# First layer's neighbourhood attention: query tiles of 8 rows by 16 columns, key blocks of 12 rows by 32 columns

## The chip, the cores and the metric

The kernel runs on one core of a Trainium2 chip. The metric is the device time of one execution in microseconds. Before the change it is 2199.93 us, the median of three runs (2194.26 to 2201.35).

## What is computed

Two layers over 1,024 latent tokens (a grid of 16 rows by 64 columns) and 256 context tokens, width 1,024. In each layer one input projection gives q, k, v and a gate z; a mixer gives y; `(y * silu(z)) @ w_out` is added to the stream and normalised. The first layer's mixer is a neighbourhood attention with 16 heads of 64. A query at row r, column w sees 8 rows by 16 columns of keys, clamped to the grid, and all 256 context keys:

```
row_start = clip(r - 4, 0, 16 - 8)
col_start = clip(w - 8, 0, 64 - 16)
s_loc = q . k_win * scale + rpb[h, r0 + i - r + 7, col_start + j - w + 15]
s_ctx = q . kc * scale
p = softmax(concat(s_loc, s_ctx))
y = p_loc @ v_win + p_ctx @ vc
```

Context queries attend to context keys alone. The second layer is a differential attention over all keys, with a rotary embedding on latent tokens.

## The kernel before

The first layer's projection and attention run in eight chunks of two heads. In a chunk PE makes twelve products (four blocks v, k, q, gate; three groups of 512, 512 and 256 tokens; L450), each in three passes over high and low parts of h and w. The v block is transposed tile by tile (L461), k and q are split into high and low parts on DVE (`split_k`, `split_q` L602, L606). Four products of the next chunk run at the end of a chunk (`ahead`).

**Items.** An item is one head and one tile of 128 queries: two rows of 64 columns. Per head there are eight local items and two of context queries, 20 items a chunk. A local item's keys are the 8 or 9 full rows that its two query rows' windows cover, 512 or 576 keys, besides 256 context keys. So it has 1,536 or 1,664 score columns (each key twice, for k's high and low part) in six matmuls (L907), a key block of 128 is transposed on PE (L917) and evacuated by ACT (L802), and multiplied with v (L930, two records for each block): 6 or 7 blocks.

DVE takes the maximum (L837) of the context scores, adds the bias to the local ones and takes their maximum in one instruction (L843), joins both maxima (L846), and after ACT's exponential (L795) takes the reciprocal (L852) and multiplies (L855). PE's order in iteration i is: scores of item i+2, first part of the transposes of i, first values of i-1, second transposes, second values. DVE's order is: normalise i, maximum of i+2. The scores of an item wait for the exponential of the item two before. `gate_y` (L862) multiplies the finished y with half the gate.

**Bias.** A table expanded in DRAM (`toeplitz`, 14 of 16 heads at the start of this stage, by POOL's queue, L220) holds for each query column a row of relative biases. For each chunk two DMAs (`load_bias`, L736) bring two heads of it into `aux`; four additions on POOL (L777, L781) put the window's mask on it. DVE waits for these (`bias_ready`) before the first maximum of a chunk.

**SP's queue.** It is strictly in order. In a chunk: late modulation loads 3 to 5 (`late.load`, L252), the next chunk's first weight block (L409), loads 6 and 7, the store of the modulation row (L283), three weight blocks, the next chunk's loads 0 to 2, then the wait for the last maximum of the chunk, `load_bias` of the next one, the wait for y, y's store (L756). The late modulation multiplies a part of w_mod with the condition on DVE, in two parts (loads 0 to 2 at the head of a chunk, 3 to 7 ahead of `split_q`; L261, L265); PE reduces it (L272) after the ninth product and before the two early gate products. The order of the start of this stage is: masks, `load_bias(0)`, weight blocks 2 and 3, late loads.

```
sp.wait_ge(max_done, CREDIT + c * NI + NI)
load_bias(c + 1)
...
sp.wait_ge(y_ready, CREDIT + c * YG + YG)
sp.dma_start(y_out[bass.ds(c * P, P), :], m.y[:, :]).then_inc(y_stored, 16)
```

## Time and profile before

| what | value |
|---|---|
| median of three runs | 2199.93 us (2194.26 to 2201.35) |
| span of the profiled execution | 2192.7 us |
| instructions in it | 32,602 |
| busy share of the span | PE 91%, DVE 59%, ACT 42%, POOL 6% |
| first layer's projection and attention, eight chunks | 941 us |
| granted TensorE clock, mean | 0.969 |

The profile lists the span of its execution, from the first to the last instruction; the times of the three runs also hold what lies around the span. Busy time of an engine is the time in which at least one of its instructions ran; matmuls overlap, so a matmul's own duration is longer than the distance to the next one's start. A bracket behind a row gives the idle time before it and what ended it. SPq is the DMA queue of SyncE; its rows are the issue of a transfer, not the transfer.

### The profile page before, as it was taken

To read this page: it belongs to the slowest core of one execution; us is meant where nothing else is said; L and a number is where in the kernel's file an instruction comes from. 1 tells how busy PE (TensorE), PEld (TensorE's weight loads), DVE (VectorE), ACT (ScalarE), POOL (GpSimd) and SP (SyncE) were. 2 spreads that over 40 slices of the span, in tenths; PEclk is the share of its full clock that TensorE was granted. 3 is DMA by queue.
4 is the path that set the end of the run, shared out by engine and by line. 5 is a ranking of instruction groups with operands and counts; after the bars stand their busy time and mean duration, and the time that the engine had idled before them with its cause. 6 is when DMAs were issued, how large, how long until landed. Compare 5 with 4: busy or idle time off the path is not lost. (4 is left out here: it accounts for less than half of the span.)

```text
span 2192.7 us, 32602 instructions
## 1 busy us (share of the span) xinstructions
PE 1985.7 (91%) x11889; PEld 1705.5 (78%) x11889; DVE 1292.7 (59%) x2330; ACT 921.9 (42%) x1544; POOL 138.0 (6%) x123
## 2 busy tenths in 40 slices
PE   7799999999999898997977999999999999998687
PEld 2688888888888888886766787878787878787566
DVE  2474646465564646475764748474747474747557
ACT  1353444435362625263113545454545454545410
POOL 0301010100001010100100000000000000000010
PEclk9899999999999999998988999999999999999889
DMA  7512111121212021114532000000000000001142
GB/s 281 152 30 77 29 58 47 41 65 41 65 36 66 27 64 41 53 59 143 190 111 88 20 29 19 29 19 29 19 29 19 29 19 29 19 20 39 48 173 96
DMA packets 99168, 134.07 MB, mean 61 GB/s; under 512 B 5152, under 2 KB 70848, under 8 KB 98992
## 3 DMA queue, kind: packets, MB, share of 16 engines
q1 hardware_dynamic: 89984, 101.05, 14.6%
q0 software_dynamic: 6544, 22.95, 3.4%
q10 hardware_dynamic: 2592, 9.44, 1.1%
q8 instruction: 30, 0.49, 0.1%
q14 instruction: 18, 0.15, 0.0%
HBM read 114.50 MB, written 22.84 MB: 63 GB/s over the span
## 5 line engine op out<-in xcount | busy, mean ns | idle before, releaser
L450 PE MATMUL acc<-h_hi,w_hi 128*128 128x512 f32 (+1 forms) x1408 | 518.6, 368 | 14.6 <-DVE w_lo L432 14.6
L450 PE MATMUL acc<-h_hi,w_lo 128*128 128x512 f32 (+1 forms) x1408 | 509.7, 362 | 0.0
L450 PE MATMUL acc<-h_lo,w_hi 128*128 128x512 f32 (+1 forms) x1408 | 509.0, 361 | 0.0
L450 PEld LDWEIGHTS acc<-h_hi,w_hi 128*128 128x128 f32 x1408 | 267.3, 190 | 60.0 <-DVE w_lo L432 15.4
L450 PEld LDWEIGHTS acc<-h_hi,w_lo 128*128 128x128 f32 x1408 | 266.6, 189 | 41.7
L450 PEld LDWEIGHTS acc<-h_lo,w_hi 128*128 128x128 f32 x1408 | 267.3, 190 | 37.9
L930 PE MATMUL acc<-pt,v 128*128 128x128 f32 x1792 | 247.4, 277 | 0.0
L802 ACT ACTIVATE pt<-acc 128x512 f32<-128x512 f32 (+2 forms) x288 | 143.5, 502 | 229.9 <-PE acc L917 229.3
L930 PEld LDWEIGHTS acc<-pt,v 128*128 128x128 f32 x1792 | 224.3, 194 | 0.2 <-ACT pt L802 0.2
L1156 PE MATMUL acc<-k_dup,q_stack 128*128 128x512 f32 (+1 forms) x768 | 185.5, 382 | 38.3 <-DVE q_stack L606 24.5
L1085 DVE TENSOR_REDUCE stats<-acc 128x1 f32<-128x1280 f32 x128 | 189.9, 1487 | 46.4 <-PE acc L1156 46.4
L1156 PEld LDWEIGHTS acc<-k_dup,q_stack 128*128 128x128 f32 x768 | 140.6, 198 | 78.6 <-issue 24.4
L917 PE MATMUL acc<-ident,big 128*128 128x128 f32 x896 | 147.8, 278 | 47.9 <-DVE big L855 47.8
L1177 PE MATMUL acc<-pt,v 128*128 128x128 f32 x1280 | 175.6, 278 | 0.8
L1034 ACT ACTIVATE pt<-acc 128x512 f32<-128x512 f32 (+1 forms) x192 | 100.7, 524 | 156.2 <-PE acc L1165 153.6
L1177 PEld LDWEIGHTS acc<-pt,v 128*128 128x128 f32 x1280 | 161.2, 194 | 3.2 <-issue 2.1
L1027 ACT ACTIVATE big<-acc,stats 128x1280 f32<-128x1280 f32 x96 | 127.5, 1328 | 72.1 <-DVE stats L1085 70.4
L917 PEld LDWEIGHTS acc<-ident,big 128*128 128x128 f32 x896 | 106.4, 142 | 62.7 <-issue 28.5
L795 ACT ACTIVATE big<-acc,stats 128x768 f32<-128x768 f32 (+2 forms) x160 | 133.3, 833 | 25.9 <-DVE stats L846 25.9
L907 PE MATMUL acc<-k_dup,q_stack 128*128 128x256 f32 (+1 forms) x832 | 139.1, 300 | 0.0
L1165 PE MATMUL acc<-ident,big 128*128 128x128 f32 x640 | 104.2, 278 | 25.7 <-DVE big L1098 23.9
L432 DVE TENSOR_TENSOR w_lo<-w_raw,w_hi 128x1024 fp32r<-128x1024 f32 x64 | 78.2, 1224 | 68.7 <-ACT w_hi L427 68.0
(146 smaller groups left out, 2556.5 us busy)
## 6 DMA issues: line engine op xcount, KB each, us to landing
w_raw<-in_w_in SPq DMA_DIRECT2D x64, 512.0 KB, 4.0
extra_prob<-in_w_mod SPq DMA_DIRECT2D x40, 256.0 KB, 3.1
w_raw<-y_t POOLq DMA_DIRECT2D x18, 512.0 KB, 5.6
w_raw<-in_w_out SPq DMA_DIRECT2D x16, 512.0 KB, 3.3
aux<-toeplitz SPq DMA_DIRECT2D x16, 448.0 KB, 5.6
big<-in_w_mod SPq DMA_DIRECT2D x24, 256.0 KB, 3.0
y_t<-y SPq DMA_DIRECT2D x8, 640.0 KB, 3.3
x<-big ACTq DMA_DIRECT2D x10, 512.0 KB, 2.6
```

Of the source, the lines that this page charges most:

```text
L450: mm = nc.tensor.matmul(m.bank(self.bank_of(j), w), wt[:, b % 2, k, :], ht[:, k, t0:t0 + w], start=(k == 0 and i == 0), stop=(k == KT - 1 ...
L795: nc.scalar.activation(prob[:, i % PB, 0:it.width], m.banks(2 * (i % 2), 0, it.width), ACT.Exp, bias=stat(i, 2), accum_out=stat(i, 3)).the ...
L802: nc.scalar.activation(m.pt[:, n % 3, 0:w], m.bank(4 + n % 2, w), ACT.Copy).then_inc(pt_ready, 1)
L907: mm = nc.tensor.matmul(m.psum[:, b, col:col + w], m.q_stack[:, it.head, it.qt * P:(it.qt + 1) * P], m.k_dup[:, it.head, part, key:key + w ...
L917: mm = nc.tensor.transpose(m.psum[:, 4 + n % 2, t * P:(t + 1) * P], prob[:, i % PB, (a + t) * P:(a + t + 1) * P], m.ident[:, :])
L930: mm = nc.tensor.matmul(m.psum[:, 6 + it.y_group % 2, (it.qt % 4) * P:(it.qt % 4 + 1) * P], m.v[:, it.key_tiles[a + t], :], m.pt[:, n % 3, ...
L1027: nc.scalar.activation(prob(mp, t), m.banks(3 * mp, 0, TOK), ACT.Exp, bias=stat(t, mp), accum_out=stat(t, 2 + mp)).then_inc(exp_done, 1)
L1034: nc.scalar.activation(m.pt[:, n % 4, 0:w], m.bank(6, w), ACT.Copy).then_inc(pt_ready, 1)
L1085: nc.vector.reduce_max(stat(t, mp), m.banks(3 * mp, 0, TOK), AX, negate=True).then_inc(max_done, 1)
L1156: mm = nc.tensor.matmul(m.bank(3 * mp + g, w), m.q_stack[:, mp, t * P:(t + 1) * P], m.k_dup[:, mp, part, k0:k0 + w], start=(part == 0), st ...
L1165: mm = nc.tensor.transpose(m.psum[:, 6, i * P:(i + 1) * P], prob(0, t)[:, (a + i) * P:(a + i + 1) * P], m.ident[:, :])
L1177: mm = nc.tensor.matmul(m.psum[:, 7, (t % 4) * P:(t % 4 + 1) * P], m.v[:, a + i, :], m.pt[:, n % 4, i * P:(i + 1) * P], start=(a + i == 0) ...
```

## The change

Query tiles become 8 rows by 16 columns, and each has one key block of 12 rows by 32 columns, 384 keys in three blocks of 128, in place of 512 or 576. Latent tokens are stored in cells of 4 rows by 8 columns (the host permutes x and the output, and the rotary table), so that a key block is three runs of 128 tokens, and q is regrouped by tile as it is split. v is transposed for each of the 16 places at which a block of 4 rows by 32 columns can start: 18 tiles a chunk in place of 10, in five groups (`v_turns`); they lie partly in `big`.

The scores lie in one bank (local, 384) and the next (context, 256), next to each other, so the maximum is: add of the bias over 384, then one reduction over 640. Transposes come in parts of 3 and 2 blocks. The factor 0.5 moves from `gate_y` to the evacuation of v.

The bias table in DRAM becomes eight shifted copies cut into strips of 8 columns (`shifted`), written by 8 + 8 DMAs in 32-byte pieces. For each chunk 64 DMAs of 8 partitions (48 pieces of 384 bytes each) bring it in. Masks shrink to one row and one column mask; POOL puts them on with 20 additions a chunk: sixteen that also move strips to their place (4 of 4 or 2 strips of 96 elements for each of four head and row pairs, 8 of 384 elements and 8 of 192) and four over 1,152 elements.

```diff
-PAD = 63 - (WIN_C - 1)
-RPB_W = 2 * WIN_C - 1 + 2 * PAD
-RPB_H = 2 * WIN_R - 1
-SLOTS = RPB_H - 1
-INNER = WIN_R + 1
+Q_ROWS, Q_COLS = 8, 16
+K_ROWS, K_COLS = 12, 32
+LOCAL = K_ROWS * K_COLS
+BAND, STRIP = 4, 8
+CELL = BAND * STRIP
+BANDS, STRIPS = ROWS // BAND, GRID_W // STRIP
+BAND_TOKENS = BAND * GRID_W
+ROW_BLOCKS, COL_BLOCKS, KINDS = ROWS // Q_ROWS, GRID_W // Q_COLS, 3
+K_BAND0 = [0, 1]
+K_STRIP0 = [0, 1, 3, 4]
+KIND = [0, 1, 1, 2]
+SLOT = [0, 8, 4]
+LOADED_AT, LOADED = 4, 6
+MOVES = [(0, 0, 4), (1, 2, 2), (1, 0, 2), (2, 0, 4)]
+K_BANDS, K_STRIPS = K_ROWS // BAND, K_COLS // STRIP
+PAD_R, PAD_C = 4, 16
+RPB_H = 2 * WIN_R - 1 + 2 * PAD_R
+RPB_W = 2 * WIN_C - 1 + 2 * PAD_C
+SHIFTS = (RPB_W + 1 - STRIP) // STRIP
...
-def expand_band(pool, rpb, toeplitz, h, bands):
-
-    src = rpb[h, :, 63:127]
-    pool.dma_start(toeplitz[h].rearrange("w d j -> d w j"),
-                   bass.AP(src.tensor, src.offset, [[RPB_W, RPB_H], [-1, GRID_W], [1, GRID_W]])).then_inc(bands, 16)
...
+def expand_bias(pool, rpb, shifted, heads, bands):
+
+    for c in range(STRIP):
+        src = rpb[heads, :, STRIP - 1 - c:2 * STRIP - 1 - c]
+        rows = (heads.stop - heads.start) * RPB_H
+        pool.dma_start(shifted[c, :, heads.start * RPB_H:heads.stop * RPB_H, :],
+                       bass.AP(src.tensor, src.offset, [[STRIP, SHIFTS], [RPB_W, rows], [1, STRIP]])).then_inc(bands, 16)
...
+        if l == 0:
+            self.v_turns = [(b // 2, [b * BAND_TOKENS + s0 * CELL for s0 in K_STRIP0]) for b in range(BANDS)]
+            self.v_turns += [(2, [SEQ, SEQ + P])]
+        else:
+            self.v_turns = [(g, range(t0, t0 + w, P)) for g, (t0, w) in enumerate(GROUPS)]
+        self.NV = len(self.v_turns)
+        self.turned_by = [max(i for i, t in enumerate(self.v_turns) if t[0] == g) + 1 for g in range(3)]
...
+        for n in range(2, self.NV - 1):
+            self.turn_v(pe, c, n)
+        if self.NV > 3:
+            self.product(pe, c, AHEAD + 1)
+        self.turn_v(pe, c, self.NV - 1)
+        for j in range(AHEAD + (2 if self.NV > 3 else 1), self.cum[2]):
...
+            if self.l == 0 and g < ROW_BLOCKS:
+                by_cell = lambda t: t.rearrange("p (r b n) -> p r b n", r=2, n=2 * CELL)
+                by_block = lambda t: t.rearrange("p (b r n) -> p r b n", r=2, n=2 * CELL)
+            else:
+                by_cell = by_block = lambda t: t
+            src = lambda rows: by_cell(m.y[rows, t0:t0 + w])
+            dst = lambda rows, h: by_block(m.q_stack[rows, h, t0:t0 + w])
...
-    def __init__(self, head, qt):
-        self.head, self.qt = head, qt
-        self.local = qt < LAT_TILES
-        self.rows = 0
+    def __init__(self, head, n):
+        self.head, self.n = head, n
+        self.local = n < LAT_TILES
         if self.local:
-            r = 2 * qt
-            start = [min(max(x - WIN_R // 2, 0), ROWS - WIN_R) for x in (r, r + 1)]
-            self.k0 = start[0]
-            self.rows = start[1] + WIN_R - start[0]
-            self.slot = self.k0 - r + WIN_R - 2
-        self.width = CTX + self.rows * GRID_W
-        tiles = [LAT_TILES + i for i in range(CTX_TILES)]
-        if self.local:
-            tiles += [self.k0 // 2 + i for i in range((self.rows + 1) // 2)]
-        self.key_tiles = tiles
-        self.y_group = head * 3 + qt // 4
-
-
-def neighbourhood(nc, m, stack, p, out_w, rpb, toeplitz, bands, masks_in, w_mod, mod_rows, y_out):
+            self.col, self.row = n // 2, n % 2
+            self.kind = KIND[self.col]
+            self.blocks = [(K_BAND0[self.row] + b) * COL_BLOCKS + self.col for b in range(K_BANDS)]
+        else:
+            self.blocks = []
+        self.blocks += [BANDS * COL_BLOCKS + i for i in range(CTX_TILES)]
+        self.width = len(self.blocks) * P
+        self.y_group = head * 3 + n // 4
+
+    def queries(self, q):
+        pos = (self.row * COL_BLOCKS + self.col) if self.local else self.n
+        return q[:, pos * P:(pos + 1) * P]
+
+    def keys(self, k):
+        first = K_BAND0[self.row]
+        bands = k[:, 0:SEQ].rearrange("p (b n) -> p b n", n=BAND_TOKENS)
+        cells = K_STRIP0[self.col] * CELL
+        return bands[:, first:first + K_BANDS, cells:cells + K_STRIPS * CELL]
...
-    turns = [(i, a, min(4, len(it.key_tiles) - a)) for i, it in enumerate(items) for a in range(0, len(it.key_tiles), 4)]
+    col_mask = m.window[:, 0:KINDS * K_COLS].rearrange("p (t s c) -> p t s c", t=KINDS, c=STRIP)
+    row_mask = m.window[:, KINDS * K_COLS:].rearrange("p (b i) -> p b i", b=ROW_BLOCKS)
+    bias = m.aux[:, :].rearrange("p (h b s n) -> p h b s n", h=2, b=ROW_BLOCKS, s=KINDS * K_STRIPS)
+
+    def bias_of(it):
+        s0 = SLOT[it.kind]
+        return bias[:, it.head, it.row, s0:s0 + K_STRIPS, :].rearrange("p s (g n) -> p g s n", n=CELL)
+
+    turns = [(i, a, min(3, len(it.blocks) - a)) for i, it in enumerate(items) for a in range(0, len(it.blocks), 3)]
...
+    BIAS_PARTS = [(h, b, r, s) for h in range(2) for b in range(ROW_BLOCKS) for r in range(Q_ROWS) for s in range(Q_COLS // STRIP)]
+    BL = 16 * len(BIAS_PARTS)
...
+    def local_scores(i):
+        return m.psum[:, 2 * (i % 2), 512 - LOCAL:512]
+
+    def scores_by_cell(i):
+        return local_scores(i).rearrange("p (g s n) -> p g s n", g=K_BANDS, n=CELL)
+
+    def ctx_scores(i):
+        return m.psum[:, 2 * (i % 2) + 1, 0:CTX]
+
+    def all_scores(i):
+        return m.banks(2 * (i % 2), 512 - LOCAL, 512 + CTX) if items[i].local else ctx_scores(i)
...
             def load_bias(c):
-                for half in range(2):
-
-                    src = toeplitz[bass.ds(c * 2, 2), :, 1 - half:1 - half + SLOTS, :].rearrange("h w d j -> w h (d j)")
-                    sp.dma_start(bias[64 * half:64 * half + 64, :, :], src).then_inc(bias_loaded, 16)
+                for h, b, r, s in BIAS_PARTS:
+                    p0 = r // BAND * (P // 2) + s * CELL + r % BAND * STRIP
+                    d0 = PAD_R + WIN_R - 1 + BAND * K_BAND0[b] - (b * Q_ROWS + r)
+                    rows = bass.ds(c * 2 * RPB_H + (h * RPB_H + d0), K_ROWS)
+                    src = shifted[:, 1 - s:1 - s + LOADED, rows, :].rearrange("c w d j -> c w (d j)")
+                    sp.dma_start(bias[p0:p0 + STRIP, h, b, LOADED_AT:LOADED_AT + LOADED, :], src).then_inc(bias_loaded, 16)
...
-            nc.gpsimd.memset(prob[:, :, WMAX - GRID_W:WMAX], 0.0).then_inc(pad_set, 1)
-            for h in range(2, HEADS):
-                expand_band(pool, rpb, toeplitz, h, bands)
+            expand_bias(pool, rpb, shifted, slice(2, HEADS), bands)
             pool.wait_ge(masks_loaded, 16)
             with pool.Fori(0, NCH) as c:
-                pool.wait_ge(bias_loaded, CREDIT + c * 32 + 32)
-                for h in range(2):
-                    nc.gpsimd.tensor_tensor(bias_inner[:, h, :], bias[:, h, 2 * GRID_W:2 * GRID_W + inner_w], mask_inner,
-                                            ALU.add).then_inc(bias_tmp, 1)
-                for h in range(2):
-                    pool.wait_ge(bias_tmp, CREDIT + c * 2 + (h + 1))
-                    nc.gpsimd.tensor_tensor(bias[:, h, :], bias[:, h, :], mask_all, ALU.add).then_inc(bias_ready, 1)
+                pool.wait_ge(bias_loaded, CREDIT + c * BL + BL)
+                for n in range(4):
+                    strips = bias[:, n // 2, n % 2, :, :].rearrange("p s (i c) -> p s i c", c=STRIP)
+                    for move, (kind, first, count) in enumerate(MOVES):
+                        src, dst = LOADED_AT + 2 - kind + first, SLOT[kind] + first
+                        if move:
+                            pool.wait_ge(bias_tmp, CREDIT + c * 4 * len(MOVES) + n * len(MOVES) + move)
+                        mask = col_mask[:, kind, first:first + count, :].rearrange("p s (i c) -> p s i c", i=1)
+                        nc.gpsimd.tensor_tensor(strips[:, dst:dst + count], strips[:, src:src + count],
+                                                mask.to_broadcast([P, count, K_ROWS, STRIP]), ALU.add).then_inc(bias_tmp, 1)
+                for n in range(4):
+                    pool.wait_ge(bias_tmp, CREDIT + c * 4 * len(MOVES) + len(MOVES) * (n + 1))
+                    strips = bias[:, n // 2, n % 2, :, :].rearrange("p s (i c) -> p s i c", c=STRIP)
+                    mask = row_mask[:, n % 2, :].rearrange("p (s i c) -> p s i c", s=1, c=1)
+                    nc.gpsimd.tensor_tensor(strips, strips, mask.to_broadcast([P, KINDS * K_STRIPS, K_ROWS, STRIP]), ALU.add)\
+                        .then_inc(bias_ready, 1)
...
                     nl = local_before[i]
-                    nc.vector.reduce_max(stat(i, 0), m.banks(s, 0, CTX), AX)
-                    if it.rows == INNER:
-                        b = bias_inner[:, it.head, :]
-                    else:
-                        b = bias[:, it.head, it.slot * GRID_W:(it.slot + WIN_R) * GRID_W]
-                    loc = m.banks(s, CTX, it.width)
-                    nc.vector.tensor_tensor_reduce(out=loc, in0=loc, in1=b, scale=1.0, scalar=-3e38, op0=ALU.add,
-                                                   op1=ALU.max, accum_out=stat(i, 1)).then_inc(raw_max, 1)
-                    v.wait_ge(raw_max, CREDIT + c * NL + (nl + 1))
-                    nc.vector.reduce_max(stat(i, 2), m.stats[:, (i % 4) * 8:(i % 4) * 8 + 2], AX, negate=True)\
-                        .then_inc(max_done, 1)
+                    loc = scores_by_cell(i)
+                    nc.vector.tensor_tensor(loc, loc, bias_of(it), ALU.add).then_inc(biased, 1)
+                    v.wait_ge(biased, CREDIT + c * NL + (nl + 1))
+                    nc.vector.reduce_max(stat(i, 2), all_scores(i), AX, negate=True).then_inc(max_done, 1)
...
-                    nc.vector.scalar_tensor_tensor(m.y[own, t0:t0 + w], m.psum[own, 6 + g % 2, 0:w], 0.5,
-                                                   m.gate[own, t0:t0 + w], ALU.mult, ALU.mult).then_inc(y_ready, 1)
+                    nc.vector.tensor_tensor(y, raw, gate, ALU.mult).then_inc(y_ready, 1)
...
-                    parts = [(s, 0, CTX, SEQ)]
+                    q, k = m.q_stack[:, it.head, :], m.k_dup[:, it.head, :, :]
+                    for part in range(2):
+                        mm = nc.tensor.matmul(ctx_scores(i), it.queries(q), k[:, part, SEQ:TOK],
+                                              start=(part == 0), stop=(part == 1))
                     if it.local:
-                        k0 = it.k0 * GRID_W
-                        parts += [(s, CTX, 256, k0), (s + 1, 0, (it.rows - 4) * GRID_W, k0 + 256)]
-                    for b, col, w, key in parts:
                         for part in range(2):
-                            mm = nc.tensor.matmul(m.psum[:, b, col:col + w], m.q_stack[:, it.head, it.qt * P:(it.qt + 1) * P],
-                                                  m.k_dup[:, it.head, part, key:key + w], start=(part == 0), stop=(part == 1))
+                            mm = nc.tensor.matmul(local_scores(i), it.queries(q), it.keys(k[:, part, :]),
+                                                  start=(part == 0), stop=(part == 1))
...
+                                              na_values(m, it.blocks[a + t]), m.pt[:, n % 3, t * P:(t + 1) * P],
+                                              start=(a + t == 0), stop=(a + t == len(it.blocks) - 1))
```

## Rows read from the trace of the kernel before

**Rows 1.** The profile's page, busy time of each engine in the span

```profile
PE 1985.7 (91%) x11889; PEld 1705.5 (78%) x11889; DVE 1292.7 (59%) x2330; ACT 921.9 (42%) x1544; POOL 138.0 (6%) x123
```

**Rows 2.** Windows by chunk; PE, PEld, DVE, ACT, POOL busy (count), clock, DMA

```profile
68.00:187.50 119.50, 107.67 (x692) 96.29 (x693) 66.82 (x151) 50.59 (x92) 18.73 (x19) 0.94 0.33 94
...
422.10:537.80 115.70, 109.71 (x744) 98.69 (x743) 65.95 (x154) 51.17 (x99) 6.94 (x4) 1.00 0.17 50
...
sum 941.00, PE 885.86 PEld 795.57 DVE 537.32 ACT 416.41 POOL 67.36; mean PE 110.73 PEld 99.45 DVE 67.16 ACT 52.05 POOL 8.42
```

**Rows 3.** TensorE timeline of one item: start, duration, line, operation, count

```profile
381.76 0.96 PE L907 MATMUL acc<-k_dup,q_stack 128*128 128x256 f32 x6
382.56 0.60 PE L917 MATMUL acc<-ident,big 128*128 128x128 f32 x4
382.99 1.06 PE L930 MATMUL acc<-pt,v 128*128 128x128 f32 x8
383.89 0.49 PE L917 MATMUL acc<-ident,big 128*128 128x128 f32 x3
384.21 0.83 PE L930 MATMUL acc<-pt,v 128*128 128x128 f32 x6
384.80 0.96 PE L907 MATMUL acc<-k_dup,q_stack 128*128 128x256 f32 x6
```

**Rows 4.** DVE timeline around the same item

```profile
379.71 0.43 DVE L837 TENSOR_REDUCE stats<-acc 128x1 f32<-128x256 f32 x1 [0.77 <-PE acc L907]
...
381.16 0.65 DVE L855 TENSOR_SCALAR big<-big,stats 128x832 f32<-128x832 f32 x1
...
382.76 0.42 DVE L837 TENSOR_REDUCE stats<-acc 128x1 f32<-128x256 f32 x1 [0.94 <-PE acc L907]
```

**Rows 5.** Groups by line and shape; busy us, mean ns, idle before

```profile
L1085 DVE TENSOR_REDUCE stats<-acc 128x1 f32<-128x1280 f32 x128 | 189.9, 1487 | 46.4 <-PE acc L1156 46.4
...
L606 DVE TENSOR_TENSOR q_stack<-y,q_stack 64x512 fp32r<-64x512 f32 x64 | 43.9, 686 | 2.0
...
L606 DVE TENSOR_TENSOR q_stack<-y,q_stack 64x256 fp32r<-64x256 f32 x16 | 6.7, 420 | 0.5
...
L855 DVE TENSOR_SCALAR big<-big,stats 128x768 f32<-128x768 f32 x64 | 39.7, 620 | 2.3
```

**Rows 6.** SP's queue at the end of a chunk, timeline

```profile
306.32 1.45 SPq L736 DMA_DIRECT2D aux<-toeplitz  x2
...
324.79 0.37 SPq L756 DMA_DIRECT2D y_t<-y  x1
```

**Rows 7.** Timeline of the next chunk's start, DVE and PE

```profile
345.43 1.41 DVE L265 SCALAR_TENSOR_TENSOR big<-big,cond_act 128x512 f32<-128x512 f32 x2
...
352.79 1.88 PE L272 MATMUL acc<-big,pick 128*2 128x512 f32 x4
...
367.05 0.42 DVE L837 TENSOR_REDUCE stats<-acc 128x1 f32<-128x256 f32 x1
```

**Rows 8.** SP's DMA issues by line; duration ns min/median/max, first and last start

```profile
L736 SPq DMA_DIRECT2D aux<-toeplitz x16: 601/625/719, 71.8 to 887.2; - x16
...
L409 SPq DMA_DIRECT2D w_raw<-in_w_in x64: 367/373/3722, 44.6 to 1924.8; - x64
...
L1257 SPq DMA_DIRECT2D aux<-in_ln_g x2: 432/450/467, 1019.1 to 2089.3; - x2
```

**Rows 9.** POOL's additions, by line and shape

```profile
L575 POOL TENSOR_TENSOR big<-big,aux 128x512 f32<-128x512 f32 x32 | 41.3, 1292 | 833.1 <-DVE big L564 833.1
...
L777 POOL TENSOR_TENSOR aux<-aux 128x576 f32<-128x576 f32 x16 | 22.4, 1420 | 761.4 <-DMA aux<-toeplitz 761.3
...
L781 POOL TENSOR_TENSOR aux<-aux 128x896 f32<-128x896 f32 x16 | 33.6, 2120 | 0.0
```

**Rows 10.** First chunk, SP's queue and ACT

```profile
78.70 14.97 SPq L252 DMA_DIRECT2D big<-in_w_mod  x1
...
95.96 1.06 ACT L427 ACTIVATE w_hi<-w_raw 128x1024 fp32r<-128x1024 f32 x1 [5.77 <-DMA w_raw<-in_w_in]
```

More of the change, by code:

```diff
@@ L452, in product, with turn_v @@
         mm.then_inc(self.proj, 1)
-    def turn_v(self, pe, c, g):
-        t0, w = GROUPS[g]
+    def turn_v(self, pe, c, n):
+        g, firsts = self.v_turns[n]
         pe.wait_ge(self.evac, CREDIT + c * self.cum[2] + (g + 1))
-        if g == 2:
-            pe.wait_ge(self.v_ready, CREDIT + c * 3 + 1)
-        for i in range(w // P):
-            mm = self.nc.tensor.transpose(self.m.psum[:, 4 + g % 2, i * P:(i + 1) * P],
-                                          self.m.k_raw[:, t0 + i * P:t0 + (i + 1) * P], self.m.ident[:, :])
+        if n >= 2:
+            pe.wait_ge(self.v_ready, CREDIT + c * self.NV + (n - 1))
+        for i, t0 in enumerate(firsts):
+            mm = self.nc.tensor.transpose(self.m.psum[:, 4 + n % 2, i * P:(i + 1) * P], self.m.k_raw[:, t0:t0 + P],
+                                          self.m.ident[:, :])
         mm.then_inc(self.v_turned, 1)
@@ L469, in pe_part @@
         self.product(pe, c, AHEAD)
-        self.turn_v(pe, c, 2)
-        for j in range(AHEAD + 1, self.cum[2]):
+        for n in range(2, self.NV - 1):
[4 more added lines that the diff above has]
+        for j in range(AHEAD + (2 if self.NV > 3 else 1), self.cum[2]):
             self.product(pe, c, j)
@@ L857, in gate_y @@
                 def gate_y(g):
-                    h, t0 = g // 3, (g % 3) * 512
-                    w = min(512, TOK - t0)
+                    h, part = g // 3, g % 3
                     own = slice(64 * h, 64 * h + 64)
+                    raw = m.psum[own, 6 + g % 2, :]
+                    if part < 2:
+                        raw = raw.rearrange("p (b g n) -> p b g n", b=2, n=2 * CELL)
+                        y, gate = (t[own, 0:SEQ].rearrange("p (g b n) -> p b g n", b=COL_BLOCKS, n=2 * CELL)
+                                   [:, 2 * part:2 * part + 2] for t in (m.y, m.gate))
+                    else:
+                        raw, y, gate = raw[:, 0:CTX], m.y[own, SEQ:TOK], m.gate[own, SEQ:TOK]
                     v.wait_ge(av_done, CREDIT + c * NT + (of_item[last_item[g]][-1] + 1))
-                    nc.vector.scalar_tensor_tensor(m.y[own, t0:t0 + w], m.psum[own, 6 + g % 2, 0:w], 0.5,
-                                                   m.gate[own, t0:t0 + w], ALU.mult, ALU.mult).then_inc(y_ready, 1)
+                    nc.vector.tensor_tensor(y, raw, gate, ALU.mult).then_inc(y_ready, 1)
                 def late_sums(v, c, part):
@@ L1400, in backbone, with token_order @@
                 rows1, lambda t: out[t * P:(t + 1) * P, :], LAT_TILES)
+def token_order():
+    return np.arange(SEQ).reshape(BANDS, BAND, STRIPS, STRIP).transpose(0, 2, 1, 3).reshape(-1)
 def shape_constants():
@@ L1413, in shape_constants @@
     rope = np.stack([np.cos(ang), np.sin(ang) * sign], axis=1).astype(np.float32)
-    w = np.arange(P) % GRID_W
-    start = np.clip(w - WIN_C // 2, 0, GRID_W - WIN_C)[:, None]
-    j = np.arange(GRID_W)[None]
-    cols = np.where((j >= start) & (j < start + WIN_C), 0.0, NEG).astype(np.float32)
-    every = np.repeat(cols[:, None], SLOTS, axis=1)
-    inner = np.repeat(cols[:, None], INNER, axis=1)
-    inner[:GRID_W, INNER - 1] = NEG
-    inner[GRID_W:, 0] = NEG
-    masks = np.concatenate([every.reshape(P, -1), inner.reshape(P, -1)], axis=1)
+    start = lambda x, window, n: np.clip(x - window // 2, 0, n - window)
+    window = lambda first, key, size: np.where((key >= first) & (key < first + size), 0.0, NEG)
+    q = np.arange(P)[:, None]
+    r, c = q // 64 * BAND + q % CELL // STRIP, q % 64 // CELL * STRIP + q % STRIP
+    cols = [0, 1, COL_BLOCKS - 1]
+    masks = [window(start(c + Q_COLS * b, WIN_C, GRID_W), STRIP * K_STRIP0[b] + np.arange(K_COLS)[None], WIN_C) for b in cols]
+    masks += [window(start(r + Q_ROWS * b, WIN_R, ROWS), BAND * K_BAND0[b] + np.arange(K_ROWS)[None], WIN_R)
+              for b in range(ROW_BLOCKS)]
+    masks = np.concatenate(masks, axis=1).astype(np.float32)
     return ident, rope, np.ascontiguousarray(masks)
```

106 lines of the change are left out of this document (57 added, 49 removed).

## The prediction

> **What bounds the kernel now.** I read the page's busy times first. PE leads with 91% of the span and no other engine is near it [rows 1], but busy time of pipelined matmuls says little about one stage, so I cut the span into windows. The first layer's eight chunks take 941 us of it. A chunk in the middle lasts 115.7 us, of which PE shows 109.7, DVE 66 and POOL 7, at a granted clock of 1.00, which is TensorE's 2.4 GHz level [rows 2]. So in this layer a microsecond taken from PE is a microsecond of the chunk, as long as what feeds PE keeps up. Three timelines then show what feeds it: PE's own over one item [rows 3], DVE's over the same item [rows 4], and SP's queue from the last row maximum of a chunk to the next chunk's start [rows 6, 7]. In rows 3 no idle time stands between PE's pieces; in rows 4 DVE waits 0.94 us for the scores. PE is the bound there.
>
> **Gain: PE's work per item.** In rows 3 one 9-row item goes from 381.76 to 384.80, 3.04 us: six score matmuls 0.80, four transposes 0.43, four value blocks 0.90, three transposes 0.32, three value blocks 0.59. A transpose is worth 0.11 us and a value block 0.22. The 8-row item has one block less, so 3.04 - 0.33 = 2.71 us. After the change every local item has 5 key blocks where it had 7 or 6, and 1,280 score columns where it had 1,664 or 1,536. At 2.4 columns a nanosecond, 384 columns fewer are 0.16 us. New item: scores 0.64 + 5 x 0.11 + 5 x 0.22 = 2.29 us.
>
> But DVE's answer has to come back in time. Now: scores start 381.76, DVE starts 382.76 [rows 3, 4], so 0.20 us after the scores' 0.80. From that start to the normalising multiply L855 it takes 1.45 us (379.71 to 381.16 [rows 4]). The new maximum is an add of 384 and a reduction of 640. The add lies halfway between 420 ns (256) and 686 ns (512) [rows 5], so 0.55; the reduction follows from 0.42 for 256 [rows 4] and 1.487 for 1,280 [rows 5], 0.82. With 0.04 for the semaphore between them and 0.10 for the reciprocal that is 1.51 us. The multiply over 640, from 620 ns for 768 [rows 5] less 0.07, is 0.55; handing on to PE costs 0.12. Chain: 0.64 + 0.20 + 1.51 + 0.55 + 0.12 = 3.02 us. PE asks for it one item plus one set of scores later, so an item can't be shorter than 3.02 - 0.64 = 2.4 us. That, not 2.29, is what I take. ACT's exponential and its evacuations get narrower and stay under both.
>
> About 12 of the 20 items of a chunk run in the full pattern (8 wide, 4 narrow); at the start, at the context items and at the change of head PE already waits for the chain, and little is gained. 8 x 0.64 + 4 x 0.31 + 8 x 0.1 = 7.2 us. The values' own transposes grow from 10 to 18 tiles, 8 x 0.11 = 0.9 us back. Net 6.3 us a chunk, **50 us in eight**. Bounds: if PE alone counted, 8 x (0.75 + 0.42) - 0.9 = 8.5 a chunk, 68 us; if only half the items gained, 25 us. The split of q now writes in runs of 64: PE has two whole gate products between the reduction and the scores that need q, and these cover even a doubled split, so nothing. The gate's multiply without its 0.5, and its strides: nothing, the same 64x512 shape.
>
> **Cost: 64 small loads on SP's queue.** Now the next chunk's bias is two DMAs, issued once the last maximum is taken (306.32), and y's store follows at 324.79, when y is ready [rows 6]. The change puts 64 DMAs there. Everything on SP behind them waits: y's store, the three late modulation loads, the next weights. The first to hurt is the late modulation. DVE's second part of its sums starts at 345.43, 39.1 us after 306.32, and PE's reduction of them starts at 352.79, right behind the last sum [rows 7]; there is no slack, and PE does its two early gate products behind it. Shifted by the 0.9 us of new transposes, the sums are due at 40.0. The y store with its gap (0.7) and a load's landing (3.0) come off that: **the 64 issues have 36.3 us, 0.57 us each.**
>
> What does one issue cost? The trace has no DMA of this shape (8 partitions, runs of 384 B). The old bias load, the same queue and the same register arithmetic, takes 625 ns [rows 8] and 0.82 from issue to issue (1.45 for the pair less its second issue [rows 6]), so 0.19 us lies between two. The weight load takes 373 ns, and a load in a row of back-to-back ones 450 ns [rows 8]. The row of sixty-four is nearest to the last one in how it is issued: 0.45 + 0.19 = 0.64 us, 41 us in all. Ends: 0.37 + 0.11 = 0.48 (31 us) and 0.82 (52 us). At 41, PE waits 4.7 us a chunk at the reduction.
>
> **Cost: POOL.** It had 4 additions, and gets 20: 8 of 384 elements, 8 of 192 and 4 of 1,152. POOL's rows give 2.19 ns an element and 0.16 us a call (1292, 1420 and 2120 ns for 512, 576 and 896 [rows 9]): 8 x 1.00 + 8 x 0.58 + 4 x 2.68 = 23.4 us, with the waits on its own semaphore 25. Bias ready: 41 + 2.5 to land + 25 = 68.5 us after 306.32. The first maximum is due at 60.7 (367.05 [rows 7]), with the transposes and the stall above at 66.3. So 2.2 us late, of which some 0.6 is covered by PE's late gate product: 1.6. Short inner runs of 8 could make POOL dearer; the lower bound is that nothing is late.
>
> Together 6.3 us in each of seven chunks, 44 us. The last chunk loads no bias.
>
> **First chunk.** Its 64 loads stand ahead of the third weight block. That one is awaited now already, until 95.96 [rows 10]. Issued 41 us after 71.8, where the first bias load stands [rows 8], it lands near 117, 21 us later than now; ACT's wait of 5.77 us in that row is partly under PE's products, so PE feels some 17, and POOL's expansions in 32-byte pieces compete with it (the queue was stuck for 14.97 us there before [rows 10]). I take 20; ends 9 and 31.
>
> **Sum.** 2192.7 us of span - 50 + 44 + 20 = 2206.7. The three timed runs have a median of 2199.93, 7.2 above the span of the profiled execution, so I forecast **2214 us**, 0.6% slower. 0.3%, some 6.6 us, is about what a measurement of this kernel tells from no change.
>
> The Trainium skill's page "SBUF — State Buffer", section "Who interferes with whom", says that a VectorE instruction with two SBUF inputs, or in a two-port mode, and a GpSimd instruction that reads SBUF exclude each other for the whole instruction. No row of before shows them side by side in SBUF, so nothing here bears it out or refutes it; it is the third rival.
>
> **Rivals.**
> *The loads are cheap* (faster). If an issue takes no more than 0.57 us, SP is through before the sums are due. At 0.48: 31 + 2.5 + 25 = 58.5, bias in time, no stall; the first chunk loses 9. 2199.9 - 50 + 9 = **2159 us**. For it: the weight load's 373 ns with 1,024 pieces. Against it: the 601 ns minimum of the bias load, which the new ones resemble in source and arithmetic. It decides at 0.57 us.
> *The loads are as dear as the old ones.* 52 us: 15.7 at the reduction and 1.6 for POOL make 17.3 x 7 = 121, the first chunk 31: 2199.9 - 50 + 121 + 31 = **2302 us**.
> *POOL and DVE get in each other's way.* POOL's additions move from a stretch where DVE is idle into the one with the ten sums and the split of q. If a DVE instruction has to wait for the POOL instruction that runs, ten sums wait about 0.8 us each (one of POOL's moves is 0.58 to 1.0), PE's reduction comes 8 us later, 56 us in seven chunks: **2270 us**, or 2243 with cheap loads (POOL then also meets the split of k, 12 a chunk). The skill's rule above is this mechanism.
> *The gain doesn't come*: the chain is longer than 3.02, above all for the strided reads of bias and scores; at 2.7 us an item the gain is 25 us and the forecast 2239. I count it to the forecast's range.
>
> **Chances.** Forecast's case 0.35 (2190 to 2245, its own range), cheap loads 0.27, dear loads 0.18, POOL against DVE 0.20. The range has to hold both sides: 2155 to 2310 leaves out the tails beyond the first two rivals. Faster: the cheap loads 0.26 and 0.05 of the forecast's case, 0.31. Same: 0.05. Slower: 0.64.
>
> **What would show it.** Start to start of the new loads on SP (0.64; under 0.57 or over 0.8 settles it). The start of y's store after the last maximum: 41 us, not 18.5. PE idle ahead of L272's successor, some 5 us a chunk, with DVE's sums released by a DMA. POOL's 20 additions in 25 us, and whether DVE's L265 sums keep their length and spacing of 0.7 us while they run. PE's items at 2.4 us start to start, with idle before the transposes released by DVE. The first chunk near 133 us, the second layer unchanged. The prediction is wrong at its root if loads or POOL's work lie wholly under the products, or if an item doesn't get below 2.7 us.

## The result and the profile after

The changed kernel takes **2272.07 us** (median of 4 runs, 2265.88 to 2275.67) against 2200.64 us for the kernel before on the same chip (4 runs, 2194.26 to 2202.43). The ratio is 1.0334, with a 95% interval of 1.0309 to 1.036: 3.3% slower, some 71 us. Ratios here are formed from the fast runs and not by dividing the two medians; one run below, the slowest of seven (2191.81 us), counts as slow and is left out of its kernel's ratio. The forecast was 2214 us. The direction was right, the size a fifth of what came.

The profiled execution has a span of 2264.1 us, 71.4 more than before. First the page's busy times, then windows of it: two chunks, counted from the first bias load of one chunk's end to the next (115.7 us for such a chunk before [rows 2]), and three stretches round one reduction (PE, PEld, DVE, ACT, POOL busy with counts, granted clock, DMA share, GB/s).

```profile
PE 1940.2 (86%) x11121; PEld 1630.7 (72%) x11121; DVE 1400.6 (62%) x2074; ACT 891.9 (39%) x1560; POOL 322.2 (14%) x250
```

```profile
214.60:337.05 122.45, 104.86 (x646) 90.01 (x646) 79.92 (x121) 47.48 (x100) 29.54 (x20) 0.94 0.18 50
337.05:460.31 123.26, 104.09 (x648) 89.49 (x647) 79.64 (x122) 47.47 (x100) 29.37 (x20) 0.94 0.18 49
383.60:395.20 11.60, 0.05 (x1) 0.00 (x0) 11.49 (x8) 0.38 (x1) 11.44 (x7) 0.70 0.09 23
395.20:398.70 3.50, 3.45 (x5) 0.42 (x5) 3.43 (x3) 0.00 (x0) 2.04 (x1) 0.54 0.00 0
398.70:411.00 12.30, 12.30 (x58) 10.40 (x59) 6.77 (x12) 7.43 (x6) 0.00 (x0) 1.00 0.29 86
```

Against [rows 1, 2]: PE lost 45 us of busy time and its share fell from 91 to 86%, while DVE gained 108 us although it executes 256 instructions fewer. In the chunk, PE has 5 us less to do than the 109.7 before, and yet the chunk is 7 us longer. The third window is where: for 11.6 us PE does nothing, while DVE and POOL are both busy for practically all of it.

Next the queue and engines around that place: SP (the loads and y's store), POOL's 20 additions, DVE, and PE's reduction. The number in brackets is the idle time before, with what ended it.

```profile
337.05 28.53 SPq L817 DMA_DIRECT2D aux<-shifted  x64
365.85 0.38 SPq L837 DMA_DIRECT2D y_t<-y  x1
```

```profile
366.93 19.96 POOL L862 TENSOR_TENSOR aux<-aux,window 128x384 f32<-128x384 f32 x16 [91.62 <-DMA aux<-shifted]
386.84 10.39 POOL L868 TENSOR_TENSOR aux<-aux,window 128x1152 f32<-128x1152 f32 x4
```

```profile
379.10 2.09 DVE L294 SCALAR_TENSOR_TENSOR big<-big,cond_act 128x512 f32<-128x512 f32 x2
381.23 4.80 DVE L294 SCALAR_TENSOR_TENSOR big<-extra_prob,cond_act,big 128x512 f32<-128x512 f32 x4
386.07 3.95 DVE L294 SCALAR_TENSOR_TENSOR big<-big,cond_act 128x512 f32<-128x512 f32 x2
390.05 5.14 DVE L294 SCALAR_TENSOR_TENSOR big<-extra_prob,cond_act,big 128x512 f32<-128x512 f32 x2
395.12 2.85 DVE L662 CAST q_stack<-y 64x512 fp32r<-64x512 f32 x2
398.00 1.40 DVE L666 TENSOR_TENSOR q_stack<-y,q_stack 64x512 fp32r<-64x512 f32 x2
```

```profile
395.25 3.44 PE L301 MATMUL acc<-big,pick 128*2 128x512 f32 x4 [11.60 <-DVE big L294]
```

The 64 loads are issued in 28.53 us, **0.446 us each**, and y's store follows 28.8 us after the last maximum. The view of their line for this chunk parts the 0.446 (durations in ns, least, median, most): the issue itself takes 278 ns, and 168 lie between two issues, with the register instructions that work out the address.

```profile
L817 SPq DMA_DIRECT2D aux<-shifted x64: 277/278/301, 337.0 to 365.3; - x64
L817 SPq MOVE aux<-shifted x64: 29/29/38, 337.0 to 365.2; - x64
```

POOL starts when they have landed, at 366.93, and works until 397.23. Into this fall the ten sums. Before, two of them took 1.41 us [rows 7]; now four take 4.80, and the last two 5.14, beside POOL's 1,152-element additions. As soon as POOL stops, q's subtraction is back at its 0.70 us. All ten take 16.1 us instead of 7.4 (345.43 to 352.79 [rows 7]), and they start 42.1 us after the last maximum instead of 39.1, mostly because the split of k before them is held up too. PE's reduction, which took 1.88 us [rows 7], starts after a wait of 11.6 us and takes 3.44, at a granted clock of 0.54, close to the half that is the level of 1.2 GHz.

What did work is the item. Starts of the scores, PE:

```profile
419.14 0.48 PE L986 MATMUL acc<-k_dup,q_stack 128*128 128x256 f32 x2
...
428.58 0.48 PE L986 MATMUL acc<-k_dup,q_stack 128*128 128x256 f32 x2
```

Four items in 9.44 us, 2.36 each, where 2.4 was forecast; before, a 9-row item took 3.04 and an 8-row one, as worked out, 2.71. In the first chunk TensorE's value transposes wait for the third weight block, whose load was issued only behind the 64 loads:

```profile
71.66 36.73 SPq L817 DMA_DIRECT2D aux<-shifted  x64
108.44 2.65 SPq L445 DMA_DIRECT2D w_raw<-in_w_in  x2
```

```profile
116.78 1.97 PE L497 MATMUL acc<-ident,k_raw 128*128 128x128 f32 x8 [15.47 <-ACT big L551]
```

The account of the 71.4 us: the first chunk's last maximum is 25.3 us later (214.62 against 189.28), six chunks cost 7.2 each (43.2), the last 7.7, and what follows the first layer is 4.9 us shorter. Of these, 3.9 lie between the last two stores of y in the second layer (109.0 us against 113.0), with the same 497 matmuls at a granted clock of 0.94 against 0.91; why the clock differs there is open.

### The profile page after: what moved, and what is told of

Read it like the earlier page. It is cut to its first block and busy times, and to the rows that moved or that the text cites. A ratio compares the mean times of both kernels' runs of the same rounds, so it can differ in the third digit from the quotient of the medians.

```text
span 2264.1 us, 32354 instructions
## 1 busy us (share of the span) xinstructions
PE 1940.2 (86%) x11121; PEld 1630.7 (72%) x11121; DVE 1400.6 (62%) x2074; ACT 891.9 (39%) x1560; POOL 322.2 (14%) x250
## 3 DMA queue, kind: packets, MB, share of 16 engines
q10 hardware_dynamic: 2592, 9.44, 1.0%
## 5 line engine op out<-in xcount | busy, mean ns | idle before, releaser
L486 PEld LDWEIGHTS acc<-h_hi,w_hi 128*128 128x128 f32 x1408 | 268.9, 191 | 71.4 <-DVE w_lo L468 20.7
L862 POOL TENSOR_TENSOR aux<-aux,window 128x384 f32<-128x384 f32 (+1 forms) x128 | 148.1, 1164 | 674.7 <-DMA aux<-shifted 667.2
L889 ACT ACTIVATE pt<-acc 128x256 f32<-128x256 f32 (+1 forms) x288 | 122.9, 431 | 215.2 <-PE acc L1000 214.6
L1000 PE MATMUL acc<-ident,big 128*128 128x128 f32 x704 | 131.6, 286 | 64.3 <-DVE big L934 63.6
L1260 PE MATMUL acc<-pt,v 128*128 128x128 f32 x1280 | 174.7, 277 | 0.7
L1013 PE MATMUL acc<-pt,v 128*128 128x128 f32 x1024 | 162.8, 280 | 0.0
L1260 PEld LDWEIGHTS acc<-pt,v 128*128 128x128 f32 x1280 | 160.4, 193 | 3.0 <-issue 1.9
L628 POOL TENSOR_TENSOR big<-big,aux 128x512 f32<-128x512 f32 x32 | 41.3, 1291 | 833.0 <-DVE big L617 833.0
L1000 PEld LDWEIGHTS acc<-ident,big 128*128 128x128 f32 x704 | 84.4, 145 | 94.8 <-issue 39.3
L1013 PEld LDWEIGHTS acc<-pt,v 128*128 128x128 f32 x1024 | 140.2, 197 | 0.2 <-ACT pt L889 0.2
L882 ACT ACTIVATE big<-acc,stats 128x640 f32<-128x640 f32 (+1 forms) x160 | 116.2, 726 | 27.2 <-DVE stats L926 27.2
L1248 PE MATMUL acc<-ident,big 128*128 128x128 f32 x640 | 104.1, 278 | 24.4 <-DVE big L1181 23.5
```

Of the source, the lines that this page charges most:

```text
L486: mm = nc.tensor.matmul(m.bank(self.bank_of(j), w), wt[:, b % 2, k, :], ht[:, k, t0:t0 + w], start=(k == 0 and i == 0), stop=(k == KT - 1 ...
L862: nc.gpsimd.tensor_tensor(strips[:, dst:dst + count], strips[:, src:src + count], mask.to_broadcast([P, count, K_ROWS, STRIP]), ALU.add).t ...
L882: nc.scalar.activation(prob[:, i % PB, 0:it.width], all_scores(i), ACT.Exp, bias=stat(i, 2), accum_out=stat(i, 3)).then_inc(exp_done, 1)
L889: nc.scalar.activation(m.pt[:, n % 3, 0:w], m.bank(4 + n % 2, w), ACT.Copy).then_inc(pt_ready, 1)
L1000: mm = nc.tensor.transpose(m.psum[:, 4 + n % 2, t * P:(t + 1) * P], prob[:, i % PB, (a + t) * P:(a + t + 1) * P], m.ident[:, :])
L1013: mm = nc.tensor.matmul(m.psum[:, 6 + it.y_group % 2, (it.n % 4) * P:(it.n % 4 + 1) * P], na_values(m, it.blocks[a + t]), m.pt[:, n % 3, t ...
```

## The experiments

Two theories stood. **Exclusion**: VectorE and GpSimd hold each other up while both work in SBUF; the loads are cheap. **Queue**: the 64 loads and the length of POOL's work set the loss, by what they make late.

**GpSimd's additions left out.** The bias is neither moved into its slots nor masked, and the items add the strips as loaded; four additions of 8 elements keep the semaphores. The 64 loads stay.

```
-    for move, (kind, first, count) in enumerate(MOVES): ...   # 16 moves, 4 row masks
+    few = bias[:, n // 2, n % 2, LOADED_AT, 0:STRIP]
+    nc.gpsimd.tensor_tensor(few, few, col_mask[:, 0, 0, :], ALU.add).then_inc(bias_ready, 1)
...
-        s0 = SLOT[it.kind]
+        s0 = LOADED_AT
```

> The changed kernel with POOL's 20 additions a chunk left out (four additions of 8 elements stand for them; the bias is then neither moved nor masked, and DVE adds the loaded strips). All 64 loads stay. Theory A, POOL and DVE exclude each other while an addition runs: DVE's ten late sums go back to 0.7 us each, PE's wait at the reduction L301 (11.6 us a chunk) vanishes and with it the slower clock behind it; a chunk falls from 123.3 to about 109.5 us, the whole to 2165 us (2155 to 2180). Theory B, the 64 loads and what queues behind them on SP, or their traffic, delay the sums: the wait stays above 8 us a chunk, the whole above 2250 us.

Measured: 2165.78 us, ratio 0.9859 (0.9822 to 0.9896). Stores of y, one per chunk, and DVE's sums from 200 to 900 us:

```profile
339.44 0.38 SPq L837 DMA_DIRECT2D y_t<-y  x1
...
448.66 0.38 SPq L837 DMA_DIRECT2D y_t<-y  x1
```

```profile
L294 DVE SCALAR_TENSOR_TENSOR big<-extra_prob,cond_act,big 128x512 f32<-128x512 f32 x68 | 48.1, 748 | 2.2 <-DMA extra_prob<-in_w_mod 0.7
```

PE's waits for the sums in the whole run (us, times, longest), first in the changed kernel, then here:

```profile
PE acc L301 <- DVE big L294: 83.9, 8, 11.7
PE acc L301 <- DVE big L294: 2.2, 7, 0.5
```

A chunk takes 109.2 us, and the sums 748 ns. With all 64 loads in place the change is worth 6.8 us a chunk against 116: so the steady chunks pay next to nothing for the loads (these waits are 0.3 us a chunk), and what they lost comes from POOL's additions. The first chunk still waits 14.9 us for its weights.

**The kernel before, its GpSimd additions moved into the sums.** Same four additions, same VectorE code; POOL only starts later.

```
     pool.wait_ge(bias_loaded, CREDIT + c * 32 + 32)
+    pool.wait_ge(p.k_own, CREDIT + c * 2 + 2)
```

> The kernel before, with one wait added on POOL: its four additions (7 us a chunk) begin when DVE has split k, that is in the stretch of the ten late sums, in place of the stretch where DVE is idle. Loads, transfers and the amount of work are unchanged. Theory A: the sums meet the additions (1.4 to 2.1 us each), PE waits at the reduction 4 to 6 us a chunk and loses some clock, the whole is 2235 us (2220 to 2260). If the engines don't exclude each other: 2200 us, as before, since the bias is still in time.

Measured: 2256.57 us, ratio 1.0256 (1.0225 to 1.0288), a loss of 58 us for four additions that only changed their place. DVE's and POOL's groups from 200 to 900 us, then the wait:

```profile
L265 DVE SCALAR_TENSOR_TENSOR big<-extra_prob,cond_act,big 128x512 f32<-128x512 f32 x60 | 64.0, 1107 | 1.7 <-DMA extra_prob<-in_w_mod 0.8
L265 DVE SCALAR_TENSOR_TENSOR big<-big,cond_act 128x512 f32<-128x512 f32 x24 | 31.0, 1332 | 0.2
L782 POOL TENSOR_TENSOR aux<-aux 128x896 f32<-128x896 f32 x12 | 30.5, 2559 | 0.0
L778 POOL TENSOR_TENSOR aux<-aux 128x576 f32<-128x576 f32 x12 | 25.8, 2168 | 690.2 <-DVE k_dup L590 690.2
```

```profile
PE acc L272 <- DVE big L265: 47.0, 8, 6.1
```

Both sides are stretched: POOL's 576 elements from 1420 ns [rows 9] to 2168, 896 from 2120 to 2559, the sums from 749 to 1107 and 1332. No bias load and no tile has changed here, so this is the mechanism by itself. It cost more than the 2235 us expected, within the range given. The waits of 5.9 us a chunk explain 47 us; PE's records of the reduction are 1014 ns long instead of 592, as in the changed kernel, which is another 1.7 us a chunk.

**GpSimd starts on each quarter as it lands.** Four semaphores in place of one; the moves of a quarter and its row mask follow each other.

```
-    pool.wait_ge(bias_loaded, CREDIT + c * BL + BL)
     for n in range(4):
+        pool.wait_ge(bias_loaded[n], CREDIT + c * (BL // 4) + BL // 4)
```

> The changed kernel with one semaphore for each quarter of the bias (a head and a block of rows), so that POOL starts on a quarter when its 16 loads have landed, and masks it at once. Loads and additions are the same in number and kind. Theory A: POOL starts some 10 us after the last maximum in place of 30 and is through at about 37, before the ten sums (due at 40); only the split of k meets it. PE's wait at the reduction falls from 11.6 to under 2 us a chunk; the whole comes to 2175 us (2165 to 2195), faster than before the change. Theory B: the loads end at the same time, so nothing moves, 2265 us or more.

Measured: 2194.66 us, ratio 0.9983 (0.9966 to 1.0): 77 us won back, at the upper end of what was expected, and no more than level with the kernel before. POOL's work now starts beside the products of the chunk before, where DVE has little to do, and ends 8 us after the last load is issued, not 32. Alone, it is quick; the next lines are its first quarter and, later in the same chunk, DVE's first sums and the split of k, which it still meets.

```profile
331.19 3.46 POOL L863 TENSOR_TENSOR aux<-aux,window 128x384 f32<-128x384 f32 x4 [84.70 <-DMA aux<-shifted]
334.73 2.19 POOL L867 TENSOR_TENSOR aux<-aux,window 128x1152 f32<-128x1152 f32 x1
```

```profile
L294 DVE SCALAR_TENSOR_TENSOR big<-extra_prob,cond_act,big 128x512 f32<-128x512 f32 x60 | 57.3, 996 | 1.7 <-DMA extra_prob<-in_w_mod 0.6
L639 DVE CAST k_dup<-k_raw 64x1280 fp32r<-64x1280 f32 x12 | 21.7, 1806 | 43.6 <-ACT k_raw L539 43.4
```

PE waits 16.5 us in the run for the sums, 2 a chunk, and a chunk takes 112.5 us.

**The first chunk's weights ahead of its bias.** SP sends weight blocks 2 and 3 and the first late loads before the 64 loads.

```
-    load_bias(0)
     p.load_second(sp)
     for u in range(late.AHEAD):
         late.load(sp, 0, u)
+    load_bias(0)
```

> The changed kernel with the start of the stage reordered on SP: weight blocks 2 and 3 and the first three late loads are issued ahead of the first chunk's 64 bias loads. If the first chunk loses its 25 us because the third weight block stands behind 64 loads, PE's wait of 15.5 us at the value transposes vanishes and the whole falls by 13 to 20 us, to 2255 us. If POOL's expansion of the table is what delays it, it falls by less than 5 us.

Measured: 2260.85 us, ratio 1.0276 (1.0233 to 1.0319), 11 us less than the changed kernel. The value transposes no longer wait. But PE now waits 14.7 us for the sums of the first chunk (60 to 215 us), since the later loads of the late modulation stand behind the 64: the wait moved on to the next load in the queue.

```profile
PE acc L301 <- DVE big L294: 14.7, 1, 14.7
```

The same order in the **kernel before** (the expectation speaks of 32 loads; its bias comes in two DMAs a chunk, as in [rows 6]):

> The kernel before, with the first chunk's weight blocks 2 and 3 and the three first loads of the late modulation ahead of its 32 bias loads. If the old 32 loads did hold up the first chunk's weights as the new 64 do, it gains: up to 8 us (2190 us, ratio 0.996). In the trace of before the value products and the late reduction waited for nothing in the first chunk, so the theory is that the order is worth nothing there: 2196 to 2200 us. If the bias lands too late for the first item, a loss of 5 us.

Measured: 2201.38 us, ratio 1.0018 (1.0006 to 1.003), nothing gained. The first chunk's loss therefore belongs to the change.

**Both.** Quarters, and weights first:

> POOL starts on each quarter of the bias as it lands, and the first chunk's weights are loaded ahead of the bias. If the two losses are separate (POOL against DVE in each chunk, and the weights behind the 64 loads once), they add: the kernel with quarters, 2194.7 us, less the 11.2 us that the changed kernel won by the order of its first chunk = 2183 us, ratio 0.993 (2176 to 2190). The 15.4 us wait of the value transposes in the first chunk is gone; TensorE still waits some 2 us a chunk for VectorE's sums. If the first chunk's wait only moves (the bias lands later and the first item waits for it), 2190 to 2197.

Measured: 2185.39 us, ratio 0.9939 (0.9916 to 0.9961), 9.3 us less than the quarters alone, where 11 was expected: the two gains add, though the first chunk still waits 17.2 us at the reduction.

**Without GpSimd's additions, weights first** (computes as little of the bias as the first experiment):

> The kernel that leaves out GpSimd's 20 additions (the bias is neither moved into its slots nor masked), with the first chunk's weights ahead of the bias. It is the floor for the kernel with head 0 early: 2165.8 - 11.2 = 2155 us (2148 to 2160), ratio 0.980.

Measured: 2164.84 us, ratio 0.9845 (0.9822 to 0.9869). I had expected 2155, and it can't be told from the 2165.78 without the new order. The first store of y is only 3 us earlier (227.96 against 230.96): PE waits 11.6 us for the first sums in place of 14.9 for the weights. So this order is worth 3 us there, and 9 to 11 where POOL's work also stands in the first chunk. What the interval covers of the rest I leave open.

**Head 0's bias early.** On top of both: quarters 0 and 1 are loaded once head 0's maxima are taken, so POOL adds to them under head 1's items:

```
+    sp.wait_ge(max_done, CREDIT + c * NI + LAT_TILES)
+    load_bias(c + 1, (0,))
     sp.wait_ge(max_done, CREDIT + c * NI + NI)
-    load_bias(c + 1)
+    load_bias(c + 1, (1,))
```

> As the kernel before this one in the list, and the bias of head 0 (quarters 0 and 1, 32 loads) is fetched as soon as the maxima of head 0's last image item are taken, so that GpSimd adds to it under head 1's items, and to head 1's quarters early in the next chunk. If GpSimd holds off VectorE only where both work, and VectorE's instructions in the items (an addition with PSUM, a multiplication by a column) suffer little: GpSimd is done before the sums, the wait for them is gone (16.5 us over the run now) and the chunks approach the 109.1 us of the kernel without GpSimd's additions: 2155 to 2168 us, ratio 0.983. If the items' VectorE instructions are lengthened as the sums were (+0.5 us on some ten of them per chunk, and VectorE sets the items' pace), the loss only moves: 2175 to 2190.

Measured: 2182.10 us (2158.76 to 2191.81, 7 runs), ratio 0.9892 (0.9853 to 0.9932), the lowest ratio of the kernels that compute everything, but not clear of the two nearest (0.9939 above, 0.9921 below). Its runs spread more than those of any other, and the windows from one store of y to the next show where time is lost:

```profile
218.91:328.00 109.09, 101.29 (x648) 88.08 (x647) 71.17 (x121) 47.51 (x101) 23.29 (x22) 1.00 0.20 55
328.00:441.69 113.69, 104.06 (x648) 90.96 (x647) 74.00 (x121) 47.48 (x101) 23.41 (x22) 0.97 0.19 53
```

The first reaches 109.1 us, the length of the chunk without any GpSimd addition. In the second the same 648 matmuls run, and 4.6 us are lost; the granted clock is 0.97. The low stretch is from 403 to 408 us (0.50), right after PE has waited 2.83 us for an item's multiplication on DVE, which stood behind a split of weights. A wait of 2.8 us is in the first window too, where the clock stays at 1.00; what decides between the two is open. The clock is not the whole loss: PE is busy 2.8 us longer, and the other 1.8 are longer waits for the items' multiplications on DVE (9.4 us against 7.6), which have a mean of 743 ns in the second window and 576 in the first. So both cases of the expectation are there, chunks near 109.1 us and items that VectorE holds up. By run, the time goes with the mean granted clock: 2158.76 at 0.966, 2163.48 at 0.963, 2174.86 at 0.959, 2184.09 at 0.957.

**Head 1's bias in its own chunk.** As the last kernel, but head 1's quarters are loaded in the chunk that uses them, and VectorE waits for a quarter at the first item that reads it. All of POOL's additions now lie under items, none under the sums:

```
     late.store_row(sp, c)
+    sp.wait_ge(max_done, CREDIT + c * NI)
+    load_bias(c, (1,))
```

> As the kernel with head 0 early, but head 1's quarters are loaded inside the chunk that uses them, behind the store of the modulation row (so the first chunk has 32 loads ahead of its late loads, and not 64), and VectorE waits for each quarter at the first item that reads it. All of GpSimd's additions then lie under items, none under the sums. If GpSimd costs nothing under the items: the first chunk's late reduction waits 14 us less (17.1 us now) and the chunks stay at 109 to 113 us: 2160 to 2175 us, ratio 0.985. If head 1's quarters come too late for items 10 and 11, or the weight blocks behind these 32 loads do (14.3 us later than now), each chunk loses 3 to 8 us: 2190 to 2230.

Measured: 2178.99 us (2176.96 to 2185.56), ratio 0.9921 (0.9908 to 0.9934), which can't be told from the last one. The expected 2160 to 2175 us did not come: the first chunk's wait at the reduction was to fall by 14 us from 17.1, and is still 12.6. What the run does show is which VectorE instructions suffer. Groups from 200 to 900 us:

```profile
L929 DVE TENSOR_REDUCE stats<-acc 128x1 f32<-128x640 f32 x96 | 79.1, 824 | 3.3
L937 DVE TENSOR_SCALAR big<-big,stats 128x640 f32<-128x640 f32 x96 | 65.8, 685 | 3.4
L927 DVE TENSOR_TENSOR acc<-acc,aux 128x384 f32<-128x384 f32 x96 | 54.1, 563 | 25.4 <-PE acc L992 24.7
L294 DVE SCALAR_TENSOR_TENSOR big<-extra_prob,cond_act,big 128x512 f32<-128x512 f32 x64 | 45.3, 749 | 2.0 <-DMA extra_prob<-in_w_mod 0.5
L639 DVE CAST k_dup<-k_raw 64x1280 fp32r<-64x1280 f32 x13 | 10.7, 822 | 76.9 <-ACT k_raw L539 76.7
```

The sums and the cast are back at the lengths they have when DVE works alone. The items' addition (one input in PSUM) and their reduction (from PSUM) stay at 563 and 824 ns, as in the kernel without additions. Only the multiplication from SBUF to SBUF grows, from a mean of 553 to 685 ns (and 354 to 561 ns for the context items' 256 columns); one of those beside POOL took 1.11 us. It has a price: PE's waits for these multiplications come to 70.3 us in this run and 69.6 in the last kernel's, against 63.8 without the additions.

## Why the prediction came out wrong

Point by point, by its own steps:

- **Gain, 50 us.** Right in size. The item takes 2.36 us, and the kernel without POOL's additions has chunks 6.8 us shorter, which would be 54 us in eight. The limit that I named is not the one seen: in those four items PE is busy for 9.43 of 9.44 us, and DVE waits 0.16 to 0.65 us for each item's scores. So PE's own work, which I had put at 2.29 us, is 2.36, and DVE's chain fits beside it with little to spare.
- **64 loads at 0.64 us, 4.7 us of stall a chunk.** Wrong. They take 0.446 us each, below the lower end of 0.48 and below the 0.57 that I had worked out as the limit; without POOL's additions PE waits 0.3 us a chunk for the sums. The 0.19 us for what lies between two issues was about right (0.168 measured); the issue itself, put at 0.45 us, takes 0.278. The trace of before had a row with that figure, the store of the modulation row on the same queue, and I did not use it:

```profile
L283 SPq DMA_DIRECT2D mod_rows<-pt x8: 278/284/351, 121.1 to 935.7; - x8
```

- **POOL, 25 us, 1.6 us late.** The duration was close for POOL by itself (23.3 us busy a chunk in the kernel with head 0's bias early) and is 30.3 us in the changed kernel, because it waits for DVE too. That the bias would be late was wrong: with the cheap loads it is there 60.2 us after the last maximum (397.23), and the first addition that reads it, held up with everything else, starts at 411.07. Where nothing holds it up, in the kernel without POOL's additions, that addition starts 61.2 us after the last maximum (310.63 to 371.84), so even the slowed POOL would have been in time, by 1 us.
- **First chunk, 20 us.** Right for the loads alone: without POOL's additions the last maximum of the first chunk is 12.5 us later than before (201.80 against 189.28), 19 with the 6.8 of gain added. With POOL's additions it is 25.3 + 6.8 = 32; the extra 13 us come with the additions, 4.9 of them as a wait for the sums and 3.5 as a longer wait for a split of weights.
- **The step that failed** is "Cost: POOL": it priced POOL's additions by when the bias is ready, and at nothing for what they do to DVE. That was the third rival, at a chance of 0.20. It is the case, in its variant with cheap loads, for which I had given 2243 us and 12 us a chunk. The runs show 14 us a chunk: from 109.2 to 123 us, of which 11.4 are the wait at the reduction and 1.6 its matmuls at the low clock. The remaining 1 us I can't place. Against 2243 that is 14 us more in seven chunks; the first chunk adds 23 more (32 where this variant had 9). That 2272 lies beside the rival's other figure, 2270, is chance: there 44 microseconds came from a stall behind the loads (33) and a late bias (11), and neither came.

The account with the measured terms: -54 + 7 x 14 + 32 - 5 = +71 us.

The rival's rule was at hand. The Trainium skill, page "SBUF — State Buffer", section "Who interferes with whom", says that VectorE with two SBUF inputs, or a cast, copy or tensor_scalar in a two-port mode, excludes a GpSimd instruction that reads SBUF for the length of a whole instruction, and that a reduction or an instruction with one SBUF input outside those modes does not. Every group above agrees: sums from 749 ns to 1107 and 1332 with the old kernel's additions late and to 1264 in the changed kernel's whole run, casts of k from 822 to 1806, multiplications from 553 to 685, PSUM additions and reductions unchanged at 563 and 824, and POOL stretched in its turn. The trace of before could not show it; what it did show was that POOL's additions moved from a stretch without DVE work into the ten sums, and that PE's reduction stood right behind the last of them. A mechanism with no row for or against it, on the only chain without slack, deserved more than 0.20.

## What to carry to other kernels

When GpSimd work gets longer or later, look not only at who needs its result but at which VectorE instructions run beside it, and whether one of them has no slack: four additions moved into such a place cost 58 us, and starting 20 additions earlier won 77 back. Additions that are fed by several loads should start on each part as it lands, and lie beside VectorE work that reads PSUM. For the second half the lengths of the instructions speak; the times of the two kernels that do so (0.9892 and 0.9921) are not clear of the one with quarters and weights first (0.9939). A price at a threshold (here 0.57 us an issue, between estimates of 0.48 and 0.64) is not settled by the likelier side; the chance should be split there.

## What the hardware showed that I had not expected

- A load of 8 partitions of 384-byte runs is issued from SP in 278 ns, against 601 to 719 for the old bias load [rows 8], with 0.446 us from one issue to the next in a series of 64. In the first chunk, while POOL still writes the table, the 64 take 36.73 us, 0.57 each. The steady chunks show no other cost of them.
- A sum of 512 elements beside POOL's 1,152-element additions took 2.6 us where it takes 0.75: that fits a wait for the whole of the other's instruction (2.19 us alone) better than a slower pace.
- After an idle time of 11.6 us the 3.44 us of the reduction ran at a granted clock of 0.54, close to the 1.2 GHz level. After 5.9 us, in the experiment on the kernel before, its matmuls were as long (1014 ns, against 592). Behind 2.8 us of waiting the clock fell in one chunk (0.50) and not in another, with the same instructions.
- Split of q into runs of 64: free. Its casts of 512 columns have a mean of 995 ns from 200 to 900 us of the changed kernel, which looks like the price of the stride, but 419 ns in the kernel without GpSimd's additions, with the same stride, and 420 before. It was the same exclusion.
